# Side by side high and low activation parts: two weight products of 384 and 256 columns in place of 320 and 320

## The chip, the cores and the metric

One Trainium2 chip, one of its cores. The metric is the device time of one execution in microseconds; lower is better. The kernel before took 1116.07 us (median of three runs, 1115.41 to 1116.44).

## What is computed

The reference is one inference step of a decoder layer for 256 prompt tokens and 8 x 8 sample tokens (320 in all) with D_MODEL 2048. All large products share one pattern: the normed input times a wide weight matrix.

```python
def in_projection(x, norm_g, w_in):
    h = rmsnorm(x, norm_g) @ w_in
    return jnp.split(h, [int(c) for c in np.cumsum(IN_SPLITS)[:-1]], axis=-1)
```

Its columns feed three branches: sparse attention with compressed, selected and window keys, block-sparse attention (MoBA), and attention into 256 memory tokens. Each branch is multiplied by a gate path, projected to D_MODEL, weighted by a gate per channel and summed; then comes one output projection, the residual, and a final norm. All inputs and outputs are fp32.

## The kernel before

**Split products.** TensorE works in the reduced format fp32r, so each fp32 factor is split into a high part (rounded to fp32r) and a low part (the remainder), and a product is made as high x high + high weights x low activations + low weights x high activations. A *tile* is 128 output channels of a weight matrix, 128x2048; it is worked off in 16 *blocks* of 128x128 (index `kb`). For each block the helper `part` (L1309 to L1321) issues three products into the same PSUM bank, each of 320 columns (`TOK`, all tokens):

```python
for kb in kbs:
    nc.tensor.matmul(out[:, 0:n], w_hi[:, u, kb, :], hi[:, kb, :], start=(kb == first), stop=False)
    nc.tensor.matmul(out[:, 0:n], w_hi[:, u, kb, :], lo[:, kb, :], start=False, stop=False)
    mm = nc.tensor.matmul(out[:, 0:n], w_lo[:, u, kb, :], hi[:, kb, :], start=False, stop=(kb == last))
```

Three places write the same three products out by hand (L1341, L1371, L1463). The activations are `h_hi`/`h_lo` (normed input), `m_hi`/`m_lo` (256 memory tokens), `oz_hi`/`oz_lo` (gated branch outputs, 16 heads) and `mrg_both` with its halves `mrg_hi`/`mrg_lo` (merged branches). The phi products (L1435 to L1440, 290 columns) and the memory values (L1412 to L1414, 512 columns) have loops of their own.

**Order.** The weights are a stream of 144 tiles, numbered by a pair index `j` from 0 to 71 and a half `u` of 0 or 1. Each half has its own buffers `raw`, `w_hi`, `w_lo` and, in most stages, its own PSUM bank `W[u]`. For every tile: SP loads `raw[u]`; ScalarE makes `w_hi[u]` (`split_hi`, L529) once TensorE is done with the previous tile of that half (`mm_done[u]`); VectorE makes `w_lo[u]` (`split_lo`, L806); TensorE waits for `lo_ready[u]` and for the bank, `w_free[u]`. VectorE reads out the bank in between, mostly as a product with the norm's factor `inv` (L1114, L1146, L1191). So while TensorE works on one half, the other half is prepared. The order on each engine is written out by hand.

**Stages.** Keys (`J_K`), memory (`J_MEM`), compression (`J_CMP`), queries and phi (`J_Q`, `J_PHI`), values (`J_V`), gate paths mixed with the prompt's attention (`J_Z`), first merge gate mixed with the sample's attention (`J_G0`), merging (`J_MRG`: six tiles per step, four gate tiles and two tiles with `oz`, of which each fills three banks, one per branch, read out by L1201 to L1207), and the output projection (`J_OUT`). The last two tiles have their own form (`half_part`, L1664, and `low_part`, L1670).

Of the kernel before, what the change touches and what calls it, by code (L numbers as in the profile page):

```python
# [32 lines left out]

J_K, J_MEM, J_CMP, J_Q, J_PHI, J_V, J_Z, J_G0, J_MRG, J_OUT, J_END = 0, 4, 8, 10, 16, 20, 24, 32, 40, 64, 72
# [44 lines left out]
def build(nc, A):  # L79
    ctx = ExitStack()  # L80
    with ctx:
# [22 lines left out]
        h_hi = fixed("h_hi", [P, KB, TOK], f32r)  # L104
        h_lo = fixed("h_lo", [P, KB, TOK], f32r)
# [57 lines left out]
        oz_hi = at("oz_hi", [P, HEADS, TOK], f32r, Z_)  # L163
        oz_lo = at("oz_lo", [P, HEADS, TOK], f32r, O_)
        mrg_both = at("mrg_both", [P, 2, KB, TOK], f32r, K_)
        mrg_hi, mrg_lo = mrg_both[:, 0], mrg_both[:, 1]
# [9 lines left out]
        vc_g = fixed("vc_g", [P, P])  # L176
        z_tmp = fixed("z_tmp", [P, TOK])
        p_c = at("p_c", [P, 2, P], f32, Z_ + 15 * 4 * TOK)
# [3 lines left out]
        o_rows = fixed("o_rows", [P, 2, P])  # L182
        top[0] = K_ + 5632
# [20 lines left out]
        ptb_moba = fixed("ptb_moba", [P, 2, P])  # L204
# [31 lines left out]
        raw_ready, hi_ready, lo_ready, mm_done, w_free = [two(n) for n in ("raw_ready", "hi_ready", "lo_ready", "mm_done", "w_free")]  # L236
# [563 lines left out]
        def _(dve):  # L800
# [34 lines left out]

            def key_tile(n, bk, j):
                dve.wait_ge(mm_done[n % 2], j + 2)
                nc.vector.tensor_tensor(kv_t[:, 4 + n, :], bk[:, 0:TOK], inv[:], ALU.mult).then_inc(w_free[n % 2], 1)
# [99 lines left out]
            for k in range(2):  # L938
                for u in range(2):
                    dve.wait_ge(mm_done[u], J_MEM + 2 + k)  # L940
                    nc.vector.tensor_tensor(kv_t[:, 12 + 2 * k + u, 0:N_MEM], ((S0, S1), W)[k][u][:, 0:N_MEM], inv_m[:], ALU.mult).then_inc(w_free[u], 1)
                    split_lo(u, J_MEM + 1 + k)
# [13 lines left out]
            for k in range(2):  # L956
                for u in range(2):
                    dve.wait_ge(mm_done[u], J_CMP + k + 2)
                    ch.link(nc.vector.tensor_tensor(kv_t[:, 2 * k + u, :], W[u][:, 0:TOK], inv[:], ALU.mult))
# [7 lines left out]
            def query_tile(u, j, slot):  # L967
                dve.wait_ge(mm_done[u], j + 2)
                nc.vector.scalar_tensor_tensor(slot, W[u][:, 0:TOK], SCALE, inv[:], ALU.mult, ALU.mult).then_inc(w_free[u], 1)
                split_lo(u, j + 1)  # L970
# [30 lines left out]
            for k in range(4):  # L1001
# [5 lines left out]
                dve.sem_inc(w_free[1], 1)  # L1007
                if k == 1:
# [103 lines left out]
            def z_scaled(u, i):  # L1112
                dve.wait_ge(mm_done[u], i + (J_Z + 2))
                ch.link(nc.vector.tensor_tensor(z_t[:, i * 2 + u, :], W[u][:, 0:TOK], inv[:], ALU.mult))  # L1114
# [29 lines left out]
            def gate0_scaled(u, b):  # L1144
                dve.wait_ge(mm_done[u], b + (J_G0 + 2))
                nc.vector.tensor_tensor(g0_t[:, b * 2 + u, :], W[u][:, 0:TOK], inv[:], ALU.mult).then_inc(w_free[u], 1)  # L1146
# [40 lines left out]
            for k in range(KB // 2):  # L1187
                for br in range(2):
                    for u in range(2):
                        dve.wait_ge(mm_done[u], k * 3 + (J_MRG + br + 2))  # L1190
                        nc.vector.tensor_tensor(g12[:, u, br, :], W[u][:, 0:TOK], inv[:], ALU.mult).then_inc(w_free[u], 1)  # L1191
# [3 lines left out]
                for u in range(2):  # L1195
# [4 lines left out]
                    dve.wait_ge(mrg_lo_rdy, k * 2 + (u + 1))  # L1200
# [614 lines left out]
```

## Time and profile before

| | before |
|---|---|
| median of three runs | 1116.07 us |
| the profiled execution | 1115.87 us |
| its span, first to last instruction | 1114.0 us |
| TensorE busy | 1101.1 us |
| VectorE busy | 605.9 us |
| ScalarE busy | 419.4 us |
| low parts of weights on VectorE (L806) | 325.1 us |
| high parts of weights on ScalarE (L529) | 268.1 us |

The profile is one execution. An engine's busy time is the time in which at least one of its instructions is open. Products on TensorE overlap in it, so the duration of one is longer than the distance to the next; the distance is read from the starts in order of time.

### The profile page before, as it was taken

The numbers are of one execution on the slowest core, as the hardware profiler recorded it, in microseconds if no ns is written. First come the engines' busy times: TensorE is split into PE (matmuls) and PEld (weight loads), VectorE is DVE, ScalarE is ACT, GpSimd is POOL, SyncE is SP. The second block draws the span as 40 slices with busy tenths as digits, with TensorE's granted clock in tenths as the row PEclk, the third lists the DMA queues.
The fourth block names the chain that finished last, engine by engine and source line by source line (L and its number), as shares of the span: only waits on it lengthen the run. The fifth ranks groups of instructions, "written<-read, shape, count | busy, mean of one in ns | idle before, by whom it ended". The sixth has DMA issues, their size and how long they took to land.

```text
span 1114.0 us, 19399 instructions
## 1 busy us (share of the span) xinstructions
PE 1101.1 (99%) x8020; PEld 1078.2 (97%) x8020; DVE 605.9 (54%) x884; ACT 419.4 (38%) x566; POOL 65.9 (6%) x121
## 2 busy tenths in 40 slices
PE   9999999999999999999999999999999999999996
PEld 7998999999999999999999999999999999999996
DVE  6884443536446767664545457455454454454445
ACT  6733322424335444443333344333333333333332
POOL 0024000000000000000101000000000000002220
PEclk9999999999999999999999999999999999999998
DMA  8646775544445233349788744544444444464442
GB/s 292 211 154 207 243 269 192 184 147 153 165 139 187 79 114 114 108 148 313 272 292 287 265 166 169 171 170 151 170 166 162 169 147 142 152 243 148 148 151 95
DMA packets 64081, 202.04 MB, mean 181 GB/s; under 512 B 6646, under 2 KB 35606, under 8 KB 45830
## 3 DMA queue, kind: packets, MB, share of 16 engines
q1 hardware_dynamic: 58888, 185.68, 48.7%
q0 software_dynamic: 2400, 10.89, 2.9%
q10 hardware_dynamic: 2718, 4.41, 1.1%
q8 instruction: 55, 0.90, 0.3%
q14 instruction: 20, 0.16, 0.0%
HBM read 193.61 MB, written 11.53 MB: 184 GB/s over the span
## 4 chain that ended last, share of the span: by engine, by line
PE 93%; DVE 2%; DMA 2%; SPq 1%; ACT 1%; issue 0%; DVEq 0%; POOL 0%; ACTq 0%
PE bank L1317 26%; PE bank L1319 26%; PE bank L1318 26%; PE bank L1664 1%; DVE w_lo L806 1%; PE bank L1440 1%; PE bank L1435 1%; PE bank L1350 1%; DMA raw<-in_stream 1%; PE bank L1414 1%; PE bank L1413 1%; PE bank L1412 1%; DMA x_t<-in_x_t 1%; DMA kt_mem<-in_mem_k 1%; ACT w_hi L529 1%; PE bank L1579 0%
## 5 line engine op out<-in xcount | busy, mean ns | idle before, releaser
L529 ACT ACTIVATE w_hi<-raw 128x2048 fp32r<-128x2048 f32 x140 | 268.1, 1915 | 573.3 <-PE bank L1319 528.1
L1317 PE MATMUL bank<-h_hi,w_hi 128*128 128x320 f32 x1536 | 480.4, 313 | 0.4 <-DVE w_lo L806 0.4
L1319 PE MATMUL bank<-h_hi,w_lo 128*128 128x320 f32 x1536 | 475.2, 309 | 0.0
L1318 PE MATMUL bank<-h_lo,w_hi 128*128 128x320 f32 x1536 | 475.1, 309 | 0.0
L806 DVE TENSOR_TENSOR w_lo<-raw,w_hi 128x2048 fp32r<-128x2048 f32 x140 | 325.1, 2322 | 178.1 <-ACT w_hi L529 178.1
L1317 PEld LDWEIGHTS bank<-h_hi,w_hi 128*128 128x128 f32 x1536 | 288.5, 188 | 4.5 <-issue 3.5
L1318 PEld LDWEIGHTS bank<-h_lo,w_hi 128*128 128x128 f32 x1536 | 288.6, 188 | 0.4
L1319 PEld LDWEIGHTS bank<-h_hi,w_lo 128*128 128x128 f32 x1536 | 288.4, 188 | 0.0
L1318 PE MATMUL bank<-oz_lo,w_hi 128*128 128x320 f32 x256 | 79.0, 309 | 0.0
L1317 PE MATMUL bank<-oz_hi,w_hi 128*128 128x320 f32 x256 | 79.0, 308 | 0.0
L1319 PE MATMUL bank<-oz_hi,w_lo 128*128 128x320 f32 x256 | 79.0, 308 | 0.0
L1317 PE MATMUL bank<-mrg_both,w_hi 128*128 128x320 f32 x224 | 69.1, 308 | 0.0
L1318 PE MATMUL bank<-mrg_both,w_hi 128*128 128x320 f32 x224 | 69.1, 308 | 0.0
L1319 PE MATMUL bank<-mrg_both,w_lo 128*128 128x320 f32 x224 | 69.1, 308 | 0.0
L1191 DVE TENSOR_TENSOR g<-bank,inv 128x320 f32<-128x320 f32 x32 | 15.7, 491 | 72.1 <-PE bank L1319 72.1
L1319 PEld LDWEIGHTS bank<-oz_hi,w_lo 128*128 128x128 f32 x256 | 48.1, 188 | 0.0
L1317 PEld LDWEIGHTS bank<-oz_hi,w_hi 128*128 128x128 f32 x256 | 48.1, 188 | 0.0
L1318 PEld LDWEIGHTS bank<-oz_lo,w_hi 128*128 128x128 f32 x256 | 48.1, 188 | 0.0
L1318 PEld LDWEIGHTS bank<-mrg_both,w_hi 128*128 128x128 f32 x224 | 42.1, 188 | 0.0
L1317 PEld LDWEIGHTS bank<-mrg_both,w_hi 128*128 128x128 f32 x224 | 42.1, 188 | 0.0
L1319 PEld LDWEIGHTS bank<-mrg_both,w_lo 128*128 128x128 f32 x224 | 42.1, 188 | 0.0
L1146 DVE TENSOR_TENSOR g_t<-bank,inv 128x320 f32<-128x320 f32 x16 | 7.9, 492 | 47.3 <-PE bank L1319 47.3
(347 smaller groups left out, 1128.1 us busy)
## 6 DMA issues: line engine op xcount, KB each, us to landing
raw<-in_stream SPq DMA_DIRECT2D x140, 1024.0 KB, 4.9
cmp_t<-in_cmp_pages SPq DMA_DIRECT2D x32, 128.0 KB, 4.2
kt_moba<-in_moba_k SPq DMA_DIRECT2D x16, 256.0 KB, 4.7
kt_mem<-in_mem_k SPq DMA_DIRECT2D x8, 512.0 KB, 6.1
vs_moba<-in_moba_v SPq DMA_DIRECT2D x16, 256.0 KB
vs_mem<-in_mem_v SPq DMA_DIRECT2D x8, 512.0 KB
out_win_old<-in_cache_win POOLq DMA_DIRECT2D x8, 512.0 KB, 3.7
raw<-in_stream SPq DMA_DIRECT2D x10, 256.0 KB, 9.8
```

The source lines that it names most:

```text
L529: nc.scalar.activation(w_hi[:, u], raw[:, u], ACT.Copy).then_inc(hi_ready[u], 1)
L806: nc.vector.tensor_tensor(w_lo[:, u], raw[:, u], w_hi[:, u].bitcast(f32), ALU.subtract).then_inc(lo_ready[u], 1)
L1191: nc.vector.tensor_tensor(g12[:, u, br, :], W[u][:, 0:TOK], inv[:], ALU.mult).then_inc(w_free[u], 1)
L1317: nc.tensor.matmul(out[:, 0:n], w_hi[:, u, kb, :], hi[:, kb, :], start=(kb == first), stop=False)
L1318: nc.tensor.matmul(out[:, 0:n], w_hi[:, u, kb, :], lo[:, kb, :], start=False, stop=False)
L1319: mm = nc.tensor.matmul(out[:, 0:n], w_lo[:, u, kb, :], hi[:, kb, :], start=False, stop=(kb == last))
L1350: mm = nc.tensor.matmul(W[0][:, 0:TOK], raw_a[:, kb, :], x_t[:, kb, :], start=(kb == 0), stop=(kb == KB - 1))
L1412: nc.tensor.matmul(out[:], m_hi[:, kb, rows], high, start=(kb == 0), stop=False)
L1413: nc.tensor.matmul(out[:], m_lo[:, kb, rows], high, start=False, stop=False)
L1414: mm = nc.tensor.matmul(out[:], m_hi[:, kb, rows], low, start=False, stop=(kb == KB - 1))
L1435: nc.tensor.matmul(out[:, 0:used], w_hi[:, 1, s, :], c_hi[:, s, 0:used], start=(s == 0), stop=False, skip_group_check=True)
L1440: mm = nc.tensor.matmul(out[:, 0:used], w_lo[:, 1, s, :], c_hi[:, s, 0:used], start=False, stop=(s == CMP_STRIDE - 1), skip_group_check=True)
```

## The change

The high and low part of an activation block now lie side by side: 640 elements per block, high in 0 to 319, low in 320 to 639. The first product by a block of high weights takes columns 0 to 383, that is, all of the high part and the first 64 columns of the low part, and writes bank columns 0 to 383. The second takes the other 256 columns of the low part and adds them to bank columns 64 to 319. The third, with the low weights, is as before. At the end of a tile the bank holds in columns 320 to 383 the low part's contribution to columns 0 to 63. VectorE copies these 64 columns to a small tile in SBUF and adds them to the bank's columns 0 to 63, before it reads out the bank (`fold`). The products with the 256 memory tokens keep their form, in a function of their own.

To make room and strides fit, `z_t` and `o_t` are interleaved like the pair that later takes their place, `mrg_both` becomes `mrg_pair`, and the small tiles `vc_g`, `p_c` and `ptb_moba` move. The read-outs of tiles without a fold count the semaphore `folded` up instead.

```diff
+EXTRA = 64
-        h_hi = fixed("h_hi", [P, KB, TOK], f32r)
-        h_lo = fixed("h_lo", [P, KB, TOK], f32r)
+        h_pair = fixed("h_pair", [P, KB, 2 * TOK], f32r)
+        h_hi, h_lo = h_pair[:, :, 0:TOK], h_pair[:, :, TOK:2 * TOK]
+        extra = fixed("extra", [P, 2, EXTRA])
...
-        z_t = at("z_t", [P, HEADS, TOK], f32, Z_)
-        o_t = at("o_t", [P, HEADS, TOK], f32, O_)
+        zo_t = at("zo_t", [P, HEADS, 2 * TOK], f32, Z_)
+        z_t, o_t = zo_t[:, :, 0:TOK], zo_t[:, :, TOK:2 * TOK]
...
+            def fold(u, j, *pairs):
+                pairs = pairs or ((W[u], extra[:, u, :]),)
+                for bk, home in pairs:
+                    copied = nc.vector.tensor_copy(home, bk[:, TOK:TOK + EXTRA])
+                copied.then_inc(folded[u], 1)
+                dve.wait_ge(folded[u], j * 2 + 1)
+                for bk, home in pairs:
+                    added = nc.vector.tensor_tensor(bk[:, 0:EXTRA], bk[:, 0:EXTRA], home, ALU.add)
+                added.then_inc(folded[u], 1)
+                dve.wait_ge(folded[u], j * 2 + 2)
...
             def query_tile(u, j, slot):
                 dve.wait_ge(mm_done[u], j + 2)
+                fold(u, j)
                 nc.vector.scalar_tensor_tensor(slot, W[u][:, 0:TOK], SCALE, inv[:], ALU.mult, ALU.mult).then_inc(w_free[u], 1)
                 split_lo(u, j + 1)
...
                     for u in range(2):
                         dve.wait_ge(mm_done[u], k * 3 + (J_MRG + br + 2))
+                        fold(u, k * 3 + (J_MRG + br))
                         nc.vector.tensor_tensor(g12[:, u, br, :], W[u][:, 0:TOK], inv[:], ALU.mult).then_inc(w_free[u], 1)
...
                     dve.wait_ge(mrg_lo_rdy, k * 2 + (u + 1))
+                    fold(u, k * 3 + (J_MRG + 2), (banks[0], extra[:, u, :]), (banks[1], bt[:, 1, 0:EXTRA]), (banks[2], bt[:, 2, 0:EXTRA]))
                     nc.vector.scalar_tensor_tensor(bt[:, 0, :], g0_t[:, k * 2 + u, :], 1.0, banks[0][:, 0:TOK], ALU.add, ALU.mult)
...
-            def part(u, j, hi, lo, n, kbs, out=None, first=0, last=KB - 1, spare=False):
-
+            def block(out, u, kb, pair, start, stop):
+                w = w_hi[:, u, kb, :]
+                nc.tensor.matmul(out[:, 0:TOK + EXTRA], w, pair[:, kb, 0:TOK + EXTRA], start=start, stop=False, skip_group_check=True)
+                nc.tensor.matmul(out[:, EXTRA:TOK], w, pair[:, kb, TOK + EXTRA:2 * TOK], start=False, stop=False, skip_group_check=True)
+                return nc.tensor.matmul(out[:, 0:TOK], w_lo[:, u, kb, :], pair[:, kb, 0:TOK], start=False, stop=stop, skip_group_check=True)
+
+            def part(u, j, pair, kbs, out=None, first=0, last=KB - 1, spare=False):
                 if kbs[0] == 0:
                     pe.wait_ge(lo_ready[u], j + 2)
                     if not spare:
                         pe.wait_ge(w_free[u], j + 1)
                 out = W[u] if out is None else out
                 for kb in kbs:
-                    nc.tensor.matmul(out[:, 0:n], w_hi[:, u, kb, :], hi[:, kb, :], start=(kb == first), stop=False)
-                    nc.tensor.matmul(out[:, 0:n], w_hi[:, u, kb, :], lo[:, kb, :], start=False, stop=False)
-                    mm = nc.tensor.matmul(out[:, 0:n], w_lo[:, u, kb, :], hi[:, kb, :], start=False, stop=(kb == last))
+                    mm = block(out, u, kb, pair, kb == first, kb == last)
                 if kbs[-1] == KB - 1:
                     mm.then_inc(mm_done[u], 1)
```

`fold` stands in the same way ahead of the read-outs of the key, value, compression, gate path and output tiles. All calls of `part` with `h`, `oz` and `mrg`, and the three places written out by hand, now use `block`.

## Rows read from the trace of the kernel before

**Rows 1.** The page's busy times, and the core's span with its mean clock.

```profile
PE 1101.1 (99%) x8020; PEld 1078.2 (97%) x8020; DVE 605.9 (54%) x884; ACT 419.4 (38%) x566; POOL 65.9 (6%) x121
...
core 0: 1114.0 us, clock 0.996
```

**Rows 2.** The page's chain that ended last, shares by engine and by line.

```profile
PE 93%; DVE 2%; DMA 2%; SPq 1%; ACT 1%; issue 0%; DVEq 0%; POOL 0%; ACTq 0%
PE bank L1317 26%; PE bank L1319 26%; PE bank L1318 26%; PE bank L1664 1%; DVE w_lo L806 1%; PE bank L1440 1%; PE bank L1435 1%; PE bank L1350 1%; DMA raw<-in_stream 1%; PE bank L1414 1%; PE bank L1413 1%; PE bank L1412 1%; DMA x_t<-in_x_t 1%; DMA kt_mem<-in_mem_k 1%; ACT w_hi L529 1%; PE bank L1579 0%
```

**Rows 3.** The line of the low weight parts, who waited for it: us, times.

```profile
  PE bank L1317: 0.7, 2
```

**Rows 4.** Groups by line and shape: count | busy us, mean ns | idle before.

```profile
L1317 PE MATMUL bank<-h_hi,w_hi 128*128 128x320 f32 x1536 | 480.4, 313 | 0.4 <-DVE w_lo L806 0.4
...
L1317 PE MATMUL bank<-oz_hi,w_hi 128*128 128x320 f32 x256 | 79.0, 308 | 0.0
L1317 PE MATMUL bank<-mrg_both,w_hi 128*128 128x320 f32 x224 | 69.1, 308 | 0.0
...
L1341 PE MATMUL bank<-h_hi,w_hi 128*128 128x320 f32 x16 | 5.6, 353 | 0.0
...
L1371 PE MATMUL bank<-h_hi,w_hi 128*128 128x320 f32 x16 | 5.1, 316 | 0.0
...
L1463 PE MATMUL bank<-h_hi,w_hi 128*128 128x320 f32 x16 | 5.0, 315 | 0.0
```

**Rows 5.** TensorE in order of time (start us, duration us), 22 products of 320 columns.

```profile
869.84 0.31 PE L1317 MATMUL bank<-h_hi,w_hi 128*128 128x320 f32 x1
...
872.92 0.31 PE L1317 MATMUL bank<-h_hi,w_hi 128*128 128x320 f32 x1
```

**Rows 6.** The same view, 28 products of 256 columns (memory keys).

```profile
82.83 0.28 PE L1318 MATMUL bank<-m_lo,w_hi 128*128 128x256 f32 x1
...
85.89 0.28 PE L1318 MATMUL bank<-m_lo,w_hi 128*128 128x256 f32 x1
```

**Rows 7.** The same view, 19 products of 290 columns (phi).

```profile
276.56 0.29 PE L1435 MATMUL bank<-c_hi,w_hi 128*128 128x290 f32 x1
...
278.97 0.30 PE L1435 MATMUL bank<-c_hi,w_hi 128*128 128x290 f32 x1
```

**Rows 8.** The same view, 19 products of 512 columns (memory values).

```profile
107.80 0.40 PE L1414 MATMUL bank<-w_lo,m_hi 128*128 128x512 f32 x1
...
111.92 0.39 PE L1414 MATMUL bank<-w_lo,m_hi 128*128 128x512 f32 x1
```

**Rows 9.** VectorE in order of time, three steps of 64 columns that read PSUM.

```profile
576.06 0.22 DVE L1166 TENSOR_TENSOR o_t<-bank,o_win 128x64 f32<-128x64 f32 x1
...
583.80 0.22 DVE L1154 COPY ptb_moba<-bank 128x64 f32<-128x64 f32 x1
583.93 0.22 DVE L1154 COPY ptb_mem<-bank 128x64 f32<-128x64 f32 x1
```

**Rows 10.** VectorE in order of time in the merging stage [idle before <-releaser].

```profile
841.44 0.49 DVE L1191 TENSOR_TENSOR g<-bank,inv 128x320 f32<-128x320 f32 x1 [2.74 <-PE bank L1319]
843.45 2.29 DVE L806 TENSOR_TENSOR w_lo<-raw,w_hi 128x2048 fp32r<-128x2048 f32 x1 [1.52 <-ACT w_hi L529]
848.48 0.49 DVE L1191 TENSOR_TENSOR g<-bank,inv 128x320 f32<-128x320 f32 x1 [2.74 <-PE bank L1319]
...
855.52 0.49 DVE L1201 SCALAR_TENSOR_TENSOR bt<-g_t,bank 128x320 f32<-128x320 f32 x1 [2.74 <-PE bank L1319]
...
857.78 2.28 DVE L806 TENSOR_TENSOR w_lo<-raw,w_hi 128x2048 fp32r<-128x2048 f32 x1
...
862.56 0.49 DVE L1201 SCALAR_TENSOR_TENSOR bt<-g_t,bank 128x320 f32<-128x320 f32 x1 [2.10 <-PE bank L1319]
```

**Rows 11.** ScalarE in order of time, the high part in the same stretch.

```profile
855.58 1.92 ACT L529 ACTIVATE w_hi<-raw 128x2048 fp32r<-128x2048 f32 x1 [4.76 <-PE bank L1319]
```

**Rows 12.** VectorE in order of time, a read-out among the prompt's softmaxes.

```profile
425.02 0.49 DVE L1114 TENSOR_TENSOR z_t<-bank,inv 128x320 f32<-128x320 f32 x1 [0.72 <-PE bank L1319]
```

More of the change, by code:

```diff
@@ L182, in build @@
         o_rows = fixed("o_rows", [P, 2, P])
+        ptb_moba = fixed("ptb_moba", [P, 2, P])
         top[0] = K_ + 5632
@@ L1340, in second_tile @@
                     pe.wait_ge(lo_x, kb + 1)
-                    nc.tensor.matmul(W[1][:, 0:TOK], w_hi[:, 1, kb, :], h_hi[:, kb, :], start=(kb == 0), stop=False)
-                    nc.tensor.matmul(W[1][:, 0:TOK], w_hi[:, 1, kb, :], h_lo[:, kb, :], start=False, stop=False)
-                    mm = nc.tensor.matmul(W[1][:, 0:TOK], w_lo[:, 1, kb, :], h_hi[:, kb, :], start=False, stop=(kb == KB - 1))
+                    mm = block(W[1], 1, kb, h_pair, kb == 0, kb == KB - 1)
                 return mm
@@ L1395, in _ @@
                 pe.wait_ge(w_free[u], 3)
-                part(u, J_MEM, m_hi, m_lo, N_MEM, ALL, (S0, S1)[u], spare=True)
+                memory_keys(u, J_MEM, (S0, S1)[u])
             for u in range(2):
                 pe.wait_ge(w_free[u], 5)
-                part(u, J_MEM + 1, m_hi, m_lo, N_MEM, ALL, spare=True)
+                memory_keys(u, J_MEM + 1, W[u])
             pe.wait_ge(consts_in, 6 * 16)
@@ L1427, in _ @@
             for k in range(4):
-                part(0, J_PHI + k, h_hi, h_lo, TOK, ALL)
+                part(0, J_PHI + k, h_pair, ALL)
                 c, m = k // 2, k % 2
@@ L1452, in first_value_pair @@
             def first_value_pair():
[L1453 removed]
+                part(0, J_V, h_pair, ALL)
                 pe.wait_ge(hid_rdy, 2)
@@ L1462, in first_value_pair @@
                         pe.wait_ge(v_lo_rdy, kb // 4 + 1)
-                    nc.tensor.matmul(W[1][:, 0:TOK], w_hi[:, 1, kb, :], h_hi[:, kb, :], start=(kb == 0), stop=False)
-                    nc.tensor.matmul(W[1][:, 0:TOK], w_hi[:, 1, kb, :], h_lo[:, kb, :], start=False, stop=False)
-                    mm = nc.tensor.matmul(W[1][:, 0:TOK], w_lo[:, 1, kb, :], h_hi[:, kb, :], start=False, stop=(kb == KB - 1))
+                    mm = block(W[1], 1, kb, h_pair, kb == 0, kb == KB - 1)
                 mm.then_inc(mm_done[1], 1)
             def value_pair(k):
-                part(0, k + J_V, h_hi, h_lo, TOK, range(0, 3))
+                part(0, k + J_V, h_pair, range(0, 3))
                 turn_pair(k - 1)
-                part(0, k + J_V, h_hi, h_lo, TOK, range(3, KB))
-                part(1, k + J_V, h_hi, h_lo, TOK, ALL)
+                part(0, k + J_V, h_pair, range(3, KB))
+                part(1, k + J_V, h_pair, ALL)
             def prompt_scores(i):
@@ L1663, in half_part @@
                 for kb in kbs:
-                    mm = nc.tensor.matmul(out, w_hi[:, u, kb, :], mrg_both[:, :, kb, h * HALF:(h + 1) * HALF], start=(kb == 0), stop=(kb == KB - 1))
+                    mm = nc.tensor.matmul(out, w_hi[:, u, kb, :], mrg_pair[:, kb, :].rearrange("p (s t) -> p s t", s=2)[:, :, h * HALF:(h + 1) * HALF], start=(kb == 0), stop=(kb == KB - 1))
                 if kbs[-1] == KB - 1:
```

90 lines of the change are left out of this document (52 added, 38 removed).

## The prediction

> **What bounds the kernel now.** I read the page's shares of busy time first, then the chain of waits, then the groups of instructions by shape, then the order in time of TensorE and VectorE. TensorE is busy in 1101.1 of 1114.0 us and its mean granted clock is 0.996 of full speed, which is the 2.4 GHz level [rows 1]. The chain that ended last lies on TensorE for 93%, and three lines of one helper, L1317 to L1319, take 26% each [rows 2]. Over the whole run, L1317 waited for the low parts of the weights only 0.7 us in two waits [rows 3]. So the time is what TensorE needs to start its products one after the other. All that counts is the distance from one start to the next, which I read off starts in order of time. The duration printed for one product (309 ns and more) is its latency, overlaps with its neighbours and is of no use here.
>
> A tile of weights is 16 blocks of 3 products. The products have one form almost everywhere, 128x320. There are 1536, 256 and 224 of them at L1317 for the three activations, and 16 more each at L1371, L1463 and L1341, each standing for three products [rows 4]. The 16 at L1341 are interleaved with the loading of the inputs, and I leave them out. 1536 + 256 + 224 + 16 + 16 = 2048 blocks remain.
>
> **What one product costs by its width.** In each stretch I divide the time between the first and last start shown by the number of steps. 320 columns: 869.84 to 872.92 us, 21 steps, 146.7 ns. 256 columns: 82.83 to 85.89, 27 steps, 113.3 ns. 290 columns: 276.56 to 278.97, 18 steps, 133.9 ns. 512 columns: 107.80 to 111.92, 18 steps, 228.9 ns [rows 5 to 8]. At 2.4 GHz, with one column a cycle, the columns alone are 133.3, 106.7, 120.8 and 213.3 ns. What is left over is 13.4 ns (320), 6.6 (256), 13.1 (290) and 15.6 (512). So a surplus of 13 to 16 ns goes with each of the wider products and half of it with the 256-wide one. The other three lie on one line (0.428 ns per column plus 9.7), and 256 lies 6 ns below it. The trace doesn't say why.
>
> **The change part by part.** (1) The first two products of a block. Before: 2 x 146.7 = 293.4 ns. After: one of 384 columns and one of 256. There is no product of this kind with 384 columns in the trace. Between the rows of 320 and 512 its surplus is 13.4 + (64/192) x 2.2 = 14.1 ns, so 160.0 + 14.1 = 174.1 ns. For 256 I take the row of 256: 113.3. The sum is 287.4 ns, 6.0 ns less per block. Over 2048 blocks that is 12.3 us. The columns streamed are the same (640), so the gain is only the surplus that the 256-wide product doesn't pay. The third product stays at 320. Each product keeps a weight load of its own, 8020 of each before [rows 1], and their number does not change.
>
> Bounds for this unknown. From below: the 384-wide product pays only the smallest surplus seen, 6.6, so the pair is 166.6 + 113.3 = 279.9, which is 13.5 ns less per block, 27.6 us. From above: the 384-wide one pays the surplus of 512 (15.6) and the 256-wide one that of 320 (13.4), so 175.6 + 120.1 = 295.7, which is 2.3 ns more, 4.7 us. I take the interpolation for 384, since it lies nearer to 320 than to 512 and 290 and 320 agree within 0.3 ns. I take the row of 256 for 256, since it is the same operation with the same number of columns.
>
> The Trainium skill speaks against this: "TensorE: Matmul & The Clock Gate", in its sections "Wait — 56ns, not 53.3ns?" and "Back-to-back issue gap", gives an isolated matmul N / 2.4 GHz plus a fixed 2.5 ns whatever N is. The trace disagrees on both counts, with 6.6 ns at 256 and 13.4 at 320. By that rule the pair would cost the same before and after, and the time would not move; that is the first rival below.
>
> (2) The spare columns on VectorE. Each tile of products with `h` or `mrg` gets a copy of 64 columns from PSUM, a wait, an addition of 64 columns into PSUM, and a wait. A copy of 64 columns out of PSUM is 0.22 us, an addition with one operand in PSUM 0.22 [rows 9]. The trace has no addition that writes PSUM; I take 0.22 for it, and even 0.5 would change nothing below. Waits between steps of VectorE are short: five chained steps take the 2.26 us from 855.52 to 857.78, less than 5 x 0.49 [rows 10]. With 0.03 us for each wait, an estimate from that, a fold is 0.5 us. What is queued behind it is the scaled read-out of the bank (0.49) and the low part of the weights (2.29). The low part waits for ScalarE's high part in any case: in a plain tile VectorE idles 1.52 us between the read-out and it [rows 10]. The fold fits in there with 1.0 us to spare, and costs nothing. In total VectorE gets some 120 x 0.5 = 60 us more on 605.9, still far from full.
>
> (3) The merging tiles have three banks, so three copies, a wait, three additions, a wait. Copies follow each other at 0.13 us [rows 9], so it is 2 x (0.22 + 2 x 0.13 + 0.03) = 1.0 us. Here nothing covers it: VectorE's five steps run from 855.52 and the low part begins at 857.78, directly after them; ScalarE's high part was done at 855.58 + 1.92 = 857.50 [rows 10, 11]. The low part then ends at 857.78 + 1.0 + 2.28 = 861.1 in place of 860.1. TensorE takes it up when the tile of the other half ends, at about 862.5 (VectorE's next read-out starts at 862.56) [rows 10]. With tiles of 6.94 us (7.04 less 16 x 6.0 ns; read-outs start at 841.44 and 848.48) 1.3 us of the 2.4 us of slack remain. It costs nothing at the end; it only begins to cost above 2.3 us.
>
> (4) In the stage of the prompt's softmaxes, VectorE has 0.72 us of idle time before the second read-out [rows 12]. The fold of the first tile lies ahead of the low part, where ScalarE is awaited, so it doesn't reach the softmax. The fold of the second goes behind this read-out's wait and again before a low part. Nothing is late next.
>
> (5) Other edits: the paired layouts, moved small tiles, semaphores counted up where no fold is made. No added transfer, no added product: nothing. The last two tiles keep their form of products (L1664, L1670), so the tail keeps its length.
>
> Sum: 0 + 0 + 0 - 12.3 us. The profiled execution took 1115.87 us for a span of 1114.0, so 1.9 us lie around the span, and it would come to 1115.87 - 12.3 = 1103.6 with a span of 1101.7. The median of the runs is 1116.07, 0.2 above it; so 1103.8.
>
> **The rivals.** First, the small surplus of the 256-wide product belongs to the memory tokens' place or order and not to its width (it is the only place where that width occurs with this kind of operand, and there all three products have it). Then the 256-wide product costs 0.428 x 256 + 9.7 = 119.3 ns by the line of the others, the pair 119.3 + 174.1 = 293.4 ns, and the time stays at 1116.1 us. For it: four widths and only one exception. Against it: the exception holds for all four tiles of that shape, which go to four different banks, and at each of them for high, low and again high activations.
>
> Second, on the other side: both new products pay the upper bound, which happens if the surplus follows where a product starts or ends in the bank or in SBUF, and not its width. The 256-wide product would go to columns 64 to 319, no longer to the first half of the bank, and the 384-wide one would read across from the high into the low part. Then 2.3 ns more per block: 1116.07 + 4.7 = 1120.8. It decides as soon as the surpluses of the two together pass 26.8 ns, that is, the 384-wide one passes 20.2 with the 256-wide one at 6.6, or 13.4 with it at 13.4. Against it: 512-wide products cover a whole bank and pay only 15.6, and 290-wide ones also pass column 256 and pay 13.1.
>
> Third, VectorE becomes late in the merging tiles. It takes a fold of over 2.3 us, against 1.0 worked out; at 3.3 us it would cost 1 us in 16 tiles, 16 us, and eat the whole gain. Nothing in the rows speaks for such a price. Fourth, a larger gain towards the lower bound, if a width that is a multiple of 128 pays less: 1116.07 - 27.6 = 1088.5. The 512-wide product with 15.6 speaks against it.
>
> **How the numbers follow.** A measurement of this kernel can tell about 0.2% (2.2 us) from no change. Forecast, 1103.8: 0.62. Nothing changes, 1116.1: 0.18. Slower by surpluses, 1120.8: 0.12. Slower by VectorE: 0.02. Much faster: 0.06. So faster 0.68, same 0.18, slower 0.14. The range should lose no more than 2 in 10: it leaves out the slower cases and most of the much faster one and takes in the unchanged one. It goes from 1100.0 (a 384-wide product with a surplus 1.9 ns below the 14.1 taken, 2048 x 1.9 = 3.8 us) to 1117.0. The likeliest case's own range is 1100 to 1108.
>
> **What would show it.** In the profile after, starts of the 384-wide product and of the 256-wide one behind it lie 174 ns apart, those of the 256-wide and the next 113, and the third step stays at 147; a tile is 6.94 us. VectorE's busy time goes to about 665 us, ScalarE's stays. The low part of the weights in a plain merging tile still waits for ScalarE, 1.0 us in place of 1.5. If the step after the 256-wide product is 119 to 120 ns, the first or second rival holds. If TensorE's waits for the line that makes the low parts (L806 now) grow beyond 1 us in total, the third does. The prediction is wrong if 384 costs over 180 ns or 256 over 119.

## The result, and the profile after

| | before | after |
|---|---|---|
| median of six runs each | 1115.87 us | 1119.99 us |
| the profiled execution | 1115.87 us | 1119.06 us |
| its span | 1114.0 us | 1117.3 us |
| VectorE busy | 605.9 us | 669.3 us |

The kernel became slower. The ratio of the times is 1.0031, with a 95% interval of 1.0021 to 1.0042; that is 3.5 us, between 2.3 and 4.7 (the two medians of the table lie 4.1 us apart). The forecast was 1103.8 with a range of 1100 to 1117, so both the sign and the range missed.

The page of after, its busy times and the costliest groups (busy us, mean ns | idle before):

```profile
PE 1101.8 (99%) x8020; PEld 1078.7 (97%) x8020; DVE 669.3 (60%) x1206; ACT 419.9 (38%) x566; POOL 89.7 (8%) x121
...
L1338 PE MATMUL bank<-h_pair,w_hi 128*128 128x384 f32 x1584 | 540.7, 341 | 0.9 <-DVE w_lo L864 0.5
L1340 PE MATMUL bank<-h_pair,w_lo 128*128 128x320 f32 x1584 | 490.3, 310 | 0.0
...
L1339 PE MATMUL bank<-h_pair,w_hi 128*128 128x256 f32 x1584 | 441.4, 279 | 0.0
```

Beside [rows 1] and [rows 4], the widths have changed as the diff says, the number of products and weight loads hasn't (8020 of each), and TensorE is as busy as it was. The 12.3 us of gain are not there at all. TensorE in order of time, the stretch of [rows 5]:

```profile
869.99 0.34 PE L1338 MATMUL bank<-h_pair,w_hi 128*128 128x384 f32 x1
870.17 0.28 PE L1339 MATMUL bank<-h_pair,w_hi 128*128 128x256 f32 x1
870.28 0.31 PE L1340 MATMUL bank<-h_pair,w_lo 128*128 128x320 f32 x1
...
872.63 0.34 PE L1338 MATMUL bank<-h_pair,w_hi 128*128 128x384 f32 x1
```

Six blocks take 872.63 - 869.99 = 2.64 us, 440 ns each; before, a block was 3 x 146.7 = 440 ns. Over all blocks the median distance from a start to the next is 176 ns behind the 384-wide product, 117 behind the 256-wide one and 147 behind the 320-wide one. The pair costs 293 ns, as before. So the products explain the gain that is missing, but not the loss. For that, TensorE's waits in after (engine, line waited for: us in all, times, longest):

```profile
PE bank L1356 <- DVE m_lo L835: 2.1, 1, 2.1
PE bank L1373 <- DVE ones L816: 1.7, 1, 1.7
PE bank L1710 <- DVE y_diag L1291: 1.6, 1, 1.6
PE bank L1577 <- DMA kt_mem<-in_mem_k: 0.9, 2, 0.7
```

The first row is new. In before TensorE never waited for `m_lo`, the low part of the memory tokens; the rows on `ones` and `y_diag` stand there with the same 1.7 and 1.6. VectorE in order of time, before and then after, at the end of the key stage (57.12 and 59.30 are the same step, the low part of the same weight tile):

```profile
57.12 2.29 DVE L806 TENSOR_TENSOR w_lo<-raw,w_hi 128x2048 fp32r<-128x2048 f32 x1 [0.92 <-ACT w_hi L529]
...
64.57 2.28 DVE L806 TENSOR_TENSOR w_lo<-raw,w_hi 128x2048 fp32r<-128x2048 f32 x1
66.77 0.48 DVE L838 TENSOR_TENSOR kv_t<-bank,inv 128x320 f32<-128x320 f32 x1
67.17 3.25 DVE L833 SCALAR_TENSOR_TENSOR m_lo<-m_t,gains,m_hi 128x256 fp32r<-128x256 f32 x8
```

```profile
59.30 2.29 DVE L808 TENSOR_TENSOR w_lo<-raw,w_hi 128x2048 fp32r<-128x2048 f32 x1
...
67.27 2.28 DVE L808 TENSOR_TENSOR w_lo<-raw,w_hi 128x2048 fp32r<-128x2048 f32 x1
69.47 0.21 DVE L841 COPY extra<-bank 128x64 f32<-128x64 f32 x1
69.72 0.23 DVE L845 TENSOR_TENSOR bank<-bank,extra 128x64 f32<-128x64 f32 x1
69.98 0.49 DVE L855 TENSOR_TENSOR kv_t<-bank,inv 128x320 f32<-128x320 f32 x1
70.39 3.25 DVE L835 SCALAR_TENSOR_TENSOR m_lo<-m_t,gains,m_hi 128x256 fp32r<-128x256 f32 x8
```

and the first product of the memory keys on TensorE, before and after:

```profile
70.47 0.40 PE L1317 MATMUL bank<-m_hi,w_hi 128*128 128x256 f32 x1
```

```profile
73.69 0.39 PE L1356 MATMUL bank<-m_hi,w_hi 128*128 128x256 f32 x1 [2.14 <-DVE m_lo L835]
```

Before, `m_lo` was done at 67.17 + 3.25 = 70.42 us, and TensorE took it up at 70.47: 0.05 us of slack. After, a fold (a copy, an addition, the gaps between: 0.52 us) stands ahead of the read-outs of key tiles 1 to 7; tile 0 has none. VectorE has little idle time left to take them. All engines in stretches of 6 us, VectorE's busy time is the third (us; then TensorE's granted clock, share of DMA, GB/s), before:

```profile
56.00:62.00 6.00, 6.00 (x43) 6.00 (x42) 5.05 (x5) 1.08 (x1) 3.06 (x6) 1.00 0.68 201
62.00:68.00 6.00, 6.00 (x43) 6.00 (x42) 5.90 (x9) 1.92 (x1) 0.00 (x0) 1.00 0.33 130
```

and after:

```profile
56.00:62.00 6.00, 6.00 (x43) 6.00 (x42) 5.95 (x12) 1.92 (x1) 3.72 (x7) 1.00 0.75 258
62.00:68.00 6.00, 6.00 (x43) 6.00 (x42) 5.85 (x7) 1.92 (x1) 0.00 (x0) 1.00 0.55 176
68.00:74.00 6.00, 3.86 (x29) 3.70 (x28) 5.93 (x13) 1.91 (x1) 0.00 (x0) 1.00 0.51 173
```

Before, VectorE had 0.95 us free in 56 to 62 and 0.10 in 62 to 68. In the order of the kernel, the folds of key tiles 1 to 6 stand ahead of the last `m_lo` steps and that of tile 7 behind them, so 6 x 0.52 = 3.1 us come in their way. The 0.92 us that VectorE idled before 57.12 are gone in after, so about 1 us is absorbed; the rest arrives at TensorE as 2.1 us of wait.

By stages, measured between the same products of the two profiled executions: the head, from TensorE's first product to the first one of the norm's gains, 21.62 us before and 22.55 after; from there to the memory keys 47.13 and 49.42; to the first phi product 164.77 and 164.39; the merging stage to the end 309.7 in both. Of the span's 3.3 us more, 2.3 lie at the memory keys and 0.9 in the head, which the experiments take up.

### The profile page after: what moved, and what is told of

It reads as the page before. It is cut to its first block, busy times and chain, and to the rows that moved or that the text cites. A ratio compares the mean times of both kernels' runs of the same rounds, so it can differ in the third digit from the quotient of the medians.

```text
span 1117.3 us, 19755 instructions
## 1 busy us (share of the span) xinstructions
PE 1101.8 (99%) x8020; PEld 1078.7 (97%) x8020; DVE 669.3 (60%) x1206; ACT 419.9 (38%) x566; POOL 89.7 (8%) x121
## 4 chain that ended last, share of the span: by engine, by line
PE 90%; DVE 3%; DMA 3%; SPq 2%; issue 1%; ACT 0%; POOL 0%; DVEq 0%; ACTq 0%
PE bank L1338 30%; PE bank L1340 25%; PE bank L1339 20%; DMA raw<-in_stream 2%; DMA kt_mem<-in_mem_k 1%; DVE w_lo L808 1%; PE bank L1696 1%; PE bank L1469 1%; PE bank L1474 1%; PE bank L1356 1%; PE bank L1448 1%; PE bank L1447 1%; PE bank L1357 1%; PE bank L1358 1%; PE bank L1446 1%
## 5 line engine op out<-in xcount | busy, mean ns | idle before, releaser
L1338 PE MATMUL bank<-h_pair,w_hi 128*128 128x384 f32 x1584 | 540.7, 341 | 0.9 <-DVE w_lo L864 0.5
L1340 PE MATMUL bank<-h_pair,w_lo 128*128 128x320 f32 x1584 | 490.3, 310 | 0.0
L1339 PE MATMUL bank<-h_pair,w_hi 128*128 128x256 f32 x1584 | 441.4, 279 | 0.0
L1338 PEld LDWEIGHTS bank<-h_pair,w_hi 128*128 128x128 f32 x1584 | 297.6, 188 | 6.7 <-issue 4.0
L1339 PEld LDWEIGHTS bank<-h_pair,w_hi 128*128 128x128 f32 x1584 | 297.8, 188 | 0.5
L1340 PEld LDWEIGHTS bank<-h_pair,w_lo 128*128 128x128 f32 x1584 | 297.3, 188 | 0.0
L1338 PE MATMUL bank<-oz_pair,w_hi 128*128 128x384 f32 x256 | 86.2, 337 | 0.0
L1340 PE MATMUL bank<-oz_pair,w_lo 128*128 128x320 f32 x256 | 79.2, 310 | 0.0
L1338 PE MATMUL bank<-mrg_pair,w_hi 128*128 128x384 f32 x224 | 75.4, 337 | 0.0
L1338 PEld LDWEIGHTS bank<-oz_pair,w_hi 128*128 128x128 f32 x256 | 48.1, 188 | 0.0
L1339 PEld LDWEIGHTS bank<-oz_pair,w_hi 128*128 128x128 f32 x256 | 48.0, 188 | 0.0
L1338 PEld LDWEIGHTS bank<-mrg_pair,w_hi 128*128 128x128 f32 x224 | 42.1, 188 | 0.0
L1339 PEld LDWEIGHTS bank<-mrg_pair,w_hi 128*128 128x128 f32 x224 | 42.0, 188 | 0.0
```

The source lines that it names most:

```text
L1338: nc.tensor.matmul(out[:, 0:TOK + EXTRA], w, pair[:, kb, 0:TOK + EXTRA], start=start, stop=False, skip_group_check=True)
L1339: nc.tensor.matmul(out[:, EXTRA:TOK], w, pair[:, kb, TOK + EXTRA:2 * TOK], start=False, stop=False, skip_group_check=True)
L1340: return nc.tensor.matmul(out[:, 0:TOK], w_lo[:, u, kb, :], pair[:, kb, 0:TOK], start=False, stop=stop, skip_group_check=True)
```

## The experiments

Three hypotheses on the products (a surplus is what a product costs beyond one cycle per column): A, the surplus is proportional, each column costs 1.1 cycles; B, the surplus is a fixed 32 cycles; C, 256 is a favourable width and the wider ones pay 13 to 16 ns, as predicted. A and B both give 704 cycles (293.3 ns) for the pair of 384 and 256, C gives 287.4 ns. And on the loss: the key folds (theory), against folds in another place or the new layout (rivals). Each probe of experiments 1 to 3 is one execution.

**1. What one product costs by its width.** The kernel after, and behind its last product series of 24 fp32r products into one bank, with weights and activations that lie in SBUF at that point.

```diff
+            go(mv(256, lo=320))
+            go(mv(320, lo=320))
+            go(mv(384, lo=256))
+            go(mv(512, lo=128))
```

(`go` issues the products, `mv` cuts the moving operand; further series have other widths, starts, distances between blocks, banks and stationary operands.)

> The changed kernel with a probe behind its last product: 43 series of 24 fp32r products each on TensorE (120 more ahead of them to bring the clock up), with one width, place, pitch or stationary operand varied per series; nothing reads their results, so only the probe's starts count, and the time is some 170 us longer. In the changed kernel a block's three starts lie 176, 117 and 147 ns apart (440 in all, 1056 cycles of 2.4 GHz for 960 columns), exactly what three times 146.7 gave before. Theory A: a product costs in proportion to its columns, 1.1 cycles each (384: 176 ns, 256: 117.3, 320: 146.7, so 512: 234.7). Theory B: a fixed surplus of 32 cycles for each product (256: 120.0, 384: 173.3, 512: 226.7). Theory C, that of the prediction: 256 wide is special by its width (113.3) and wider ones pay 13 to 16 ns. Under A or B the 113.3 ns of the memory products must come from something else than the width, and one of the series with another place, pitch or stationary operand should show 113 at 256 and under 146 at 320.

The first and the last line of four series (the view joins two equal products into one line, "x2"):

```profile
1137.39 0.40 PE L1751 MATMUL bank<-mrg_pair,w_hi 128*128 128x256 f32 x2
...
1139.51 0.40 PE L1751 MATMUL bank<-mrg_pair,w_hi 128*128 128x256 f32 x2
...
1149.70 0.46 PE L1751 MATMUL bank<-mrg_pair,w_hi 128*128 128x320 f32 x2
...
1152.78 0.45 PE L1751 MATMUL bank<-mrg_pair,w_hi 128*128 128x320 f32 x2
...
1157.09 0.51 PE L1751 MATMUL bank<-mrg_pair,w_hi 128*128 128x384 f32 x2
...
1160.76 0.51 PE L1751 MATMUL bank<-mrg_pair,w_hi 128*128 128x384 f32 x2
...
1175.87 0.62 PE L1751 MATMUL bank<-mrg_pair,w_hi 128*128 128x512 f32 x2
...
1180.77 0.63 PE L1751 MATMUL bank<-mrg_pair,w_hi 128*128 128x512 f32 x2
```

By 18, 21, 21 and 21 steps: 117.8, 146.7, 174.8 and 233.3 ns. From the last 20 steps of each series, and in cycles of 2.4 GHz:

| columns | 192 | 224 | 256 | 288 | 320 | 384 | 448 | 480 | 512 |
|---|---|---|---|---|---|---|---|---|---|
| ns | 111.7 | 111.7 | 117.8 | 133.2 | 146.7 | 174.7 | 202.4 | 216.7 | 233.3 |
| cycles | 268 | 268 | 283 | 320 | 352 | 419 | 486 | 520 | 560 |
| cycles over the columns | 76 | 44 | 27 | 32 | 32 | 35 | 38 | 40 | 48 |

The surplus grows from 32 cycles at 320 to 48 at 512, with a floor of 111.7 ns for narrow products. It isn't fixed, as B had it, and not quite proportional either: A's 1.1 cycles per column hold at 288, 320 and 384 (1.09 to 1.11), and at 448 and 480 it is 1.08. For this change that is one answer: 174.7 + 117.8 = 292.5 ns for the pair against 2 x 146.7 = 293.3. C is out. The rows of 512 had weights as the moving operand, and with those the probe too gives less, 227.8 ns against 233.3. 256 has several prices: 117.8 ns here, 113.35 with the output at column 64 or 256, 119.6 and 120.0 from other starts or with weights moving. The predicted 113.3 was one of these values and not the width's own. In the kernel after, the 256-wide product also writes from column 64 and costs 117, so the place of the output alone doesn't fix the price either. A repeated pattern of 384, 256 and 320 gives a mean of 146.55 ns, the price of three products of 320. For these widths the cost goes with the columns, and their number stays 640. It doesn't for every split: a pattern of 512, 128 and 320, the same 960 columns, gives a mean of 162.45 ns.

**2. The same from the side of the weights.** Is the surplus the weight load's? Narrower stationary operands, and plain fp32 products.

```diff
+            go(mv(320, lo=0), w=lambda i: (w_lo if i % 3 == 2 else w_hi)[:, 0, (i // 3) % KB, 0:32], m=32)
+            go([x.bitcast(f32) for x in mv(320, lo=0, count=12)], w=lambda i: w_hi[:, 0, (i // 3) % KB, :].bitcast(f32))
```

> The changed kernel with a second probe behind its last product: 23 series of 24 fp32r products (the last two of 12 fp32 products), results used by nothing. First the stationary operand narrowed from 128 to 96, 64 and 32 columns at 320, 512 and 256 moving columns. Theory A2, the surplus comes from the moving operand alone (1.1 cycles a column): the distances stay at 146.7, 233 and 113 to 120 ns whatever the stationary width. Theory B2, it comes from the weight load beside it: the surplus shrinks with the stationary width, to a quarter at 32 columns (136 to 137 ns at 320). Then 256 columns three times each with the output at column 0, at 64, and with another start of the moving operand: does the distance (113.3 or 117.7 before) follow the output column, or change from one repeat to the next?

With 128, 96, 64 and 32 stationary columns, 320 moving ones cost 146.65, 146.7, 146.7 and 146.65 ns. So the width of the weight load isn't in it. (At 512 moving columns the four lie between 228.3 and 233.35 ns and at 256 between 113.8 and 118.95, without an order by the stationary width.) Plain fp32 products stand in the trace as two records each, and the starts of records lie 269.1 ns apart at 320 columns and 215.9 at 256: the first is 2 x 320 + 6 cycles, the second 2 x 256 + 6. So plain fp32 has 6 cycles at either width and no surplus per column. The same probe repeats the 256-wide series of experiment 1, instruction for instruction, three times, and it gives 113.35 to 113.4 ns where experiment 1 had 117.8; from start 16 it gives 119.65 all three times. So the price of 256 columns isn't fixed by width, place and operands together, and what else is in it stays open.

**3. Places.** Does any start or cut of the moving operand make 320 cheaper?

```diff
+            go(mv(256, lo=0, base=64))
+            go(mv(320, lo=0, base=48))
```

> The changed kernel with a third probe behind its last product, 34 series of 24 fp32r products, results used by nothing: 256 columns from eleven starts of the moving operand (0 to 128 columns on), each behind a series of 320 columns, 320 columns from six more starts, 320 columns taken as 2, 5 and 10 pieces with gaps, and 448, 480 and 500 columns. Theory A2, a product pays about 0.1 cycle per moving column wherever it lies: 320 stays at 146.7 ns everywhere, 256 between 113 and 120 with its start, 448 to 500 near 1.085 cycles a column. Theory D, some placement escapes the surplus at 320: one series comes near 136 ns, and the kernel could be made faster by it.

256 columns: 117.8 ns from start 0, 116.7 to 119.6 from starts 4 to 48, 113.3 from 64, 96 and 128. 320 columns: 146.7 from every start tried here, in one piece, five or ten, 145.6 in two. Experiment 1 has 147.5 from start 1, and 145.35 as the lowest, in a series that takes its moving operand from two tensors in turn. By an estimate, 1.3 ns on 3 x 2048 products would be 8 us; so no place found gives the 12.3 us that the change was costed at, and no kernel was built on this one.

**4. No folds at all.** All folds left out (64 of the columns then miss a contribution of the low part), the semaphore counted up in their place.

```diff
             def fold(u, j, *pairs):
-                pairs = pairs or ((W[u], extra[:, u, :]),)
...
+                dve.sem_inc(folded[u], 2)
```

> The changed kernel without any copy or addition of the 64 spare columns on VectorE; the low part's contribution to columns 0 to 63 is left out of the results. Theory 1, the fold on VectorE is the whole loss and TensorE's products cost the same: 1116 us, ratio 1.000 to the kernel before. Theory 2, the products or the paired layout lose something of their own: it stays above 1.001 (1118 or more).

1116.6 us, ratio 1.0009 [1.0000, 1.0019]; from the gains' product to the memory keys 47.14 us, and the wait for `m_lo` is gone. The products are those of after, so their widths bring nothing and cost, by the interval, at most 0.2%.

**5. Only the seven key folds left out** (the other 122 tiles keep theirs).

```diff
             def key_tile(n, bk, j):
...
-                    fold(n % 2, j, (bk, extra[:, n % 2, :]))
+                    dve.sem_inc(folded[n % 2], 2)
```

> The changed kernel with the fold left out for the seven key tiles alone (their spare columns are left out of the results), all other 121 read-outs with it. Theory 1: VectorE is late only ahead of the memory keys, where TensorE waited 2.1 us for the low parts of the memory tokens; without these seven folds that wait goes, and the time falls by 2 to 2.5 us, to a ratio of about 1.001. Theory 2, the loss is spread over all folds: with 7 of some 129 gone it stays at 1.003.

1116.33 us, ratio 0.9998 [0.9988, 1.0008], 47.14 us to the memory keys. The whole loss is gone with seven of the 129 folds, of which six stand ahead of `m_lo`, though VectorE's busy time is 666.7 us.

**6. Only the key folds kept**, all others left out.

```diff
+            def key_fold(u, j, *pairs):
...
             def fold(u, j, *pairs):
+                dve.sem_inc(folded[u], 2)
...
-                    fold(n % 2, j, (bk, extra[:, n % 2, :]))
+                    key_fold(n % 2, j, (bk, extra[:, n % 2, :]))
```

> The changed kernel with the fold for the seven key tiles alone; elsewhere the copy and the addition of the 64 spare columns are left out (and with them their share of the results). Theory 1, VectorE is late only ahead of the memory keys: all of the loss is there, a ratio of 1.002 to 1.003 (1118 to 1119 us), TensorE waits some 2 us for the low parts of the memory tokens. Theory 2, the loss comes from the many other folds: 1.000.

1118.66 us, ratio 1.0020 [1.0010, 1.0030], 49.41 us to the memory keys, and TensorE's wait is back:

```profile
PE bank L1359 <- DVE m_lo L835: 2.1, 1, 2.1
```

Here another cost shows, which the profiled execution of after didn't have. TensorE in order of time behind that wait:

```profile
73.33 0.58 PE L1359 MATMUL bank<-m_hi,w_hi 128*128 128x256 f32 x1 [2.13 <-DVE m_lo L835]
73.71 0.42 PE L1360 MATMUL bank<-m_lo,w_hi 128*128 128x256 f32 x1
...
76.28 0.31 PE L1360 MATMUL bank<-m_lo,w_hi 128*128 128x256 f32 x1
76.42 0.28 PE L1361 MATMUL bank<-m_hi,w_lo 128*128 128x256 f32 x1
...
77.56 0.28 PE L1359 MATMUL bank<-m_hi,w_hi 128*128 128x256 f32 x1
```

From 73.71 to 76.28 there are 12 steps of 214 ns, from 76.42 to 77.56 ten of 114. The granted clock was at its lower level, 1.2 GHz, in these 2.6 us (0.50 of full speed in the stretch from 74 to 76 us), and 12 x 0.1 = 1.2 us went there.

```profile
74.00:76.00 2.00, 2.00 (x11) 2.00 (x11) 1.93 (x4) 0.00 (x0) 0.00 (x0) 0.50 0.00 0
```

The stretch from 68 to 90 us, in after, in this kernel, and in the kernels of experiments 1 and 2, which up to their probe are the kernel after (the clock is the 1.00, 0.92, 0.84, 0.92):

```profile
68.00:90.00 22.00, 19.86 (x168) 19.57 (x167) 18.53 (x33) 7.78 (x7) 6.17 (x11) 1.00 0.43 144
```

```profile
68.00:90.00 22.00, 19.87 (x158) 19.71 (x158) 18.04 (x33) 7.78 (x7) 6.53 (x12) 0.92 0.42 144
```

```profile
68.00:90.00 22.00, 19.85 (x147) 19.69 (x146) 16.82 (x33) 7.79 (x7) 6.55 (x12) 0.84 0.40 139
```

```profile
68.00:90.00 22.00, 19.85 (x157) 19.68 (x156) 17.80 (x33) 7.78 (x7) 6.77 (x13) 0.92 0.42 144
```

The third probe has 0.92 too. Of four profiled executions of after's own instructions, three lose clock behind the wait of 2.1 us. From the first product of the memory keys to the first phi product, the kernels whose clock falls behind this wait take 165.5 to 167.0 us, those whose clock stays 164.35 to 165.25. The unprofiled runs of after fit: three of the five have a mean clock of 0.995 and took 1119.78, 1120.19 and 1120.45 us, two have 0.996 (1119.38 and 1120.39), while the profiled one took 1119.06 at 0.997. The ten runs of this kernel fit as well: the four at 0.997 took 1117.47 to 1118.36 us, the three at 0.994 or 0.995 took 1119.41 to 1121.23. In all five kernels without a wait for `m_lo` at this point (before, and experiments 4, 5, 7 and 11) the clock stays at 1.00 there.

**7. The layout alone.** The paired layout, the first two products 320 wide again, no folds.

```diff
-                nc.tensor.matmul(out[:, 0:TOK + EXTRA], w, pair[:, kb, 0:TOK + EXTRA], start=start, stop=False, skip_group_check=True)
-                nc.tensor.matmul(out[:, EXTRA:TOK], w, pair[:, kb, TOK + EXTRA:2 * TOK], start=False, stop=False, skip_group_check=True)
+                nc.tensor.matmul(out[:, 0:TOK], w, pair[:, kb, 0:TOK], start=start, stop=False, skip_group_check=True)
+                nc.tensor.matmul(out[:, 0:TOK], w, pair[:, kb, TOK:2 * TOK], start=False, stop=False, skip_group_check=True)
```

> The changed kernel with the paired layout, but products of 320, 320 and 320 columns and no fold; it computes all of the reference. Theory 1: the same as the kernel before, ratio 1.000, tiles of 7.04 us. Theory 2, high and low part in one row of 2560 bytes conflict more or less than two separate tensors: tiles differ from 7.04 us and the time by more than 2 us.

1116.53 us, ratio 1.0011 [1.0001, 1.0021]. Beside experiment 4 (1.0009) and 5 (0.9998), which have the same layout, a cost of up to 0.1% of the layout can't be told from none; its profiled execution had the shortest head of all, 21.25 us.

**8. A longer read-out ahead of `m_lo`.** In after, three of the key tiles (4 to 6) make their read-out three times.

```diff
+                for _ in range(2 if 4 <= n <= 6 else 0):
+                    ch.link(nc.vector.tensor_tensor(kv_t[:, 4 + n, :], bk[:, 0:TOK], inv[:], ALU.mult))
```

> The changed kernel with the scaled read-out of key tiles 4, 5 and 6 made three times instead of once, each repeat after a wait for the last: six more steps of 0.5 us on VectorE ahead of the last low parts of the memory tokens, 3.1 us. Results unchanged. Theory 1, VectorE sets the start of the memory keys: the time rises by the full 3 us over the changed kernel, 1.006 against the kernel before, and TensorE's wait there goes from 2.1 to some 5.2 us. Theory 2, there is still slack: under 1 us more.

1123.05 us, ratio 1.0059 [1.0042, 1.0076]; 52.57 us to the memory keys and a wait of 5.3:

```profile
PE bank L1358 <- DVE m_lo L835: 5.3, 1, 5.3
```

Six added steps of 0.52 us (3.1 us) make the wait 3.2 us longer, and the median lies 3.1 us above that of after: what VectorE gets there beyond the folds goes to the end in full.

**9. The same load on the kernel before.**

```diff
+                for _ in range(2 if 4 <= n <= 6 else 0):
+                    ch.link(nc.vector.tensor_tensor(kv_t[:, 4 + n, :], bk[:, 0:TOK], inv[:], ALU.mult))
```

> The kernel before (products 320/320/320, no fold), with the scaled read-out of key tiles 4, 5 and 6 made three times instead of once: 3.1 us more on VectorE ahead of the last low parts of the memory tokens. In the kernel before, the last of these low parts ended at 70.42 us and TensorE took them up at 70.47. Theory 1, VectorE already had no slack there before the change: 3 us more, ratio 1.0027, TensorE waits some 3 us for them. Theory 2, the slack of over 2 us that the merging stage shows holds here too: 1 us or less.

1118.84 us, ratio 1.0020 [1.0010, 1.0030], with a wait where before had none:

```profile
PE bank L1319 <- DVE m_lo L833: 2.0, 1, 2.0
```

3.1 us added, 2.0 waited for: about 1 us is absorbed, as with the six folds, which also bring 3.1, and the clock falls behind this wait too (0.92 over 68 to 90 us). Theory 1 had expected a wait of 3 us and theory 2 at most 1; the measured one lies between. So the limit was in the kernel before already: work on VectorE there shows once it passes about 1 us, with or without the change.

**10. The read-outs moved behind `m_lo`.** Key tiles 4 to 6 go behind the second half of `m_lo`.

```diff
-            key_tile(4, key_banks[4], 2)
             dve.wait_ge(m_squared, 4)
             low_part(m_lo, m_t, m_hi, 1, 0, 8, hi_m, lo_m)
...
             low_part(m_lo, m_t, m_hi, 1, 8, 16, hi_m, lo_m)
+            key_tile(4, key_banks[4], 2)
+            key_tile(5, key_banks[5], 2)
+            key_tile(6, W[0], 3)
```

> The changed kernel, whole, with three read-outs (key tiles 4, 5 and 6, each with its fold, about 0.93 us) moved on VectorE behind the last low parts of the memory tokens. Theory 1: these low parts come 2.8 us earlier, TensorE's wait of 2.1 us goes, and the time falls back to that of the kernel before, ratio 1.000, with all folds in place. Theory 2, the folds cost something elsewhere too: it stays above 1.001.

This one missed: 1119.43 us, ratio 1.0024 [1.0014, 1.0034]. `m_lo` is in time (47.11 us to the memory keys), but the wait is only moved:

```profile
PE bank L1356 <- DVE w_lo L808: 2.3, 1, 2.3
```

The three folds and read-outs now stand ahead of the next low part of weights, which begins at 73.36 us in place of 71.19 in before, and TensorE waits for a low part until 84.64, with the clock at 0.77 from 84 to 88 us. VectorE is short of time from the keys on into the memory tiles, and this change of order doesn't take work from it; other orders were not tried.

**11. Key tiles without the pair.** Nothing is left out: key tiles in three products of 320 columns and no fold, all other tiles as in after.

```diff
+            def plain(out, u, kb, pair, start, stop):
+                w = w_hi[:, u, kb, :]
+                nc.tensor.matmul(out[:, 0:TOK], w, pair[:, kb, 0:TOK], start=start, stop=False, skip_group_check=True)
+                nc.tensor.matmul(out[:, 0:TOK], w, pair[:, kb, TOK:2 * TOK], start=False, stop=False, skip_group_check=True)
+                return nc.tensor.matmul(out[:, 0:TOK], w_lo[:, u, kb, :], pair[:, kb, 0:TOK], start=False, stop=stop, skip_group_check=True)
```

> The changed kernel, complete, but the eight key tiles use products of 320, 320 and 320 columns and so need no fold; all other tiles keep 384, 256, 320 and the fold. Theory 1: as the kernel before, ratio 1.000 within 0.001, since neither the form of the products nor the other 121 folds cost anything. Theory 2: the other folds cost something: above 1.001.

1116.34 us, ratio 1.0001 [0.9992, 1.0010]. The loss is repaired and nothing is gained: a version faster than before was not found, and by experiment 1 the pair of 384 and 256 has no gain to give.

## Why the prediction was wrong

**What bounds the kernel** held. TensorE sets the end, and the distance of starts is what counts.

**Step (1)** is where the gain failed: the term of the pair, and in it mostly the 256-wide product, priced at 113.3 ns. In the kernel its step is 117. The 384-wide product was interpolated to 174.1 ns, nearly what the probe gives by itself (174.7), and its step in the kernel is 176. The two together cost 293 ns where 287.4 were forecast, and 293.4 before; so the 6 ns per block, and with them the 12.3 us, aren't there. The signs that the prediction had set for this (384 over 180 ns, 256 over 119) didn't come: each product missed by less, and the sum still took all of the gain. Two rows that looked like widths of one series were different cases: [rows 8] has the weights as moving operand, and [rows 6] other activations in other places of SBUF. The four tiles of the memory keys, taken as evidence for the width, were one case four times. The sentence "the gain is only the surplus that the 256-wide product doesn't pay" took the price of one row for a property of the width. The first rival, which gave 293.4 ns and an unchanged time, had the sum of the pair right, with another split of it (174.1 and 119.3).

That rival's page, in the Trainium skill "TensorE: Matmul & The Clock Gate", section "Back-to-back issue gap", has N / 2.4 GHz plus a fixed 2.5 ns. It named the right outcome, equal cost of the pair, by another way. By estimates from its formula, 320 columns would take 135.8 ns and 512 columns 215.8; the traces here disagree for fp32r, with 146.7 and 233.3. For an fp32 record, taken as two cycles a column, the estimate is 269.2 ns, and there the trace agrees with 269.1.

**Step (2)** is where the loss came from: it put the cost of the folds at nothing, and the wait that it left out is 2.1 us of TensorE on `m_lo`, which delays the memory keys by 2.3. It costed a fold at 0.5 us, which the trace confirms (69.47 to 69.98), and hid it in the 1.52 us of idle time of a merging tile [rows 10]. That holds there: after shows 0.99 us left. But one stage stood for all. "In total VectorE gets some 60 us more on 605.9, still far from full" is an average; in 62 to 68 us it was full to 5.90 of 6.00. What was queued behind the key folds wasn't a low part that waits for ScalarE, it was `m_lo`, with 0.05 us of slack. The missing question was what is late next in the stage where VectorE is fullest. The third rival had the right mechanism, VectorE late, with the merging tiles as its place and 0.02 as its chance. Its sign was set on the wrong line: TensorE's waits for the low parts of the weights are 0.8 us in after, in all, under the 1 us named, and the wait that counts is for the low part of the memory tokens.

**Step (3)** held to the number: in after, copies, additions and gaps of a merging tile of three banks run from 823.57 to 824.62, 1.05 us against 1.0 worked out, and the merging stage to the end is 309.7 us in both kernels. VectorE in order of time in after:

```profile
823.57 0.23 DVE L841 COPY extra<-bank 128x64 f32<-128x64 f32 x1 [1.04 <-PE bank L1340]
823.71 0.35 DVE L841 COPY bt<-bank 128x64 f32<-128x64 f32 x2
824.09 0.23 DVE L845 TENSOR_TENSOR bank<-bank,extra 128x64 f32<-128x64 f32 x1
824.23 0.35 DVE L845 TENSOR_TENSOR bank<-bank,bt 128x64 f32<-128x64 f32 x2
824.62 0.49 DVE L1227 SCALAR_TENSOR_TENSOR bt<-g_t,bank 128x320 f32<-128x320 f32 x1
```

**Steps (4) and (5)** held in the total: experiment 5 keeps the folds of the softmax stages and the layouts and is where before is. VectorE's 669.3 us answer to the 665 forecast.

**The loss in numbers.** Against before: 2.3 us to the memory keys (shown by experiments 4 to 6 and 11), and some 1.2 us of clock in the executions where it falls. Together that is 3.5, inside the measured interval of 2.3 to 4.7; how often the clock falls in unprofiled runs is inferred from their mean clocks only, so the second part is the less certain one. In the profiled execution of after the clock did not fall, and 0.9 us of its 3.3 lie in the head. That is the spread of executions: the same head, instruction for instruction, takes 22.55 us in after and 22.15, 21.95 and 21.28 in the kernels of experiments 1 to 3, and the head spans 21.25 to 22.55 over all kernels profiled, with and without folds. It is open whether the 0.1% of experiments 4 and 7 is real, what makes fp32r pay a tenth of a cycle per column, and what sets the price of 256 columns.

## What to carry to other kernels

A saving of a few ns per product has to be measured in the very sequence of products that will run, with the same operands, place in the bank and format, before it is multiplied by thousands; two rows of other stages aren't a price list. Work that is put on an engine everywhere is costed in the stage where that engine has least idle time, by what stands queued behind it and when that is needed, since the average and the typical tile say nothing of it. A short wait of TensorE may cost more than its own length, because the clock can fall behind it: here a wait of 2.1 us was followed by 1.2 us more.

## What the runs showed that was not expected

- An fp32r product costs 1.08 to 1.11 cycles per moving column from 288 columns to 512 at 2.4 GHz, and in series of 192 and of 224 columns 111.7 ns; an fp32 record costs 2 cycles per column and 6. The number of stationary columns (32 to 128) changes nothing at 320.
- 256 columns are a case of their own: between 113.3 and 120.0 ns. Some places repeat to 0.1 ns from one probe to the next (119.6 from start 16), and one series gave 117.8 ns in one probe and 113.35 to 113.4 in another.
- At the lower clock level, the 256-wide products lie 214 ns apart, which is 256 columns at 1.2 GHz (213.3) with no surplus. Products of 320 columns in the first microseconds of the probe of experiment 1, at the same level, lie 266.6 ns apart (320 / 1.2 = 266.7). So the surplus shows at 2.4 GHz alone.
- A wait of 2.0 to 2.2 us was followed in five of six profiled executions by 1.2 GHz for some microseconds; TensorE had been busy at 2.4 GHz before it.
- VectorE adds 64 columns into PSUM in 0.23 us, as fast as it copies them out in 0.22.
- The folds outside the key stage made GpSimd's additions into `y_ss` (14 of 320 columns) three times as long: a mean of 2.6 us in every kernel with these folds, 0.88 in every kernel without. Nothing on the path waited for them; the cause was not tested.
